# Reordering the tail of a mixer layer, and two projection products moved ahead of the head loop

## Chip, cores and metric

One NeuronCore of a Trainium2 chip runs the whole program. The metric is device time in microseconds; the span is that of one profiled execution. Engines: PE (TensorE), DVE (VectorE), ACT (ScalarE), POOL (GpSimd), and SP, which only issues DMAs here.

## The reference, cut to what matters

The program computes a first block (a mixer and a mixture of 64 experts) on 256 tokens of width 1024, then two layers of a second block. The change is in the mixer:

```python
glu_in, z, xbc, dt_raw, gate_in = split(n @ w_in)
u = a * sigmoid(b)                                    # a, b = halves of glu_in
u = silu(layernorm(causal_dwconv(u, cv_dw_w, cv_dw_b)))      # 31 taps: the long convolution
y_cv = u @ w_cv_out
y = ssd(silu(causal_dwconv(xbc)), softplus(dt_raw + dt_bias), ...) + d_skip * xh
y = rmsnorm_by_group(y * silu(z))                     # 4 groups of 512 channels
y_ssm = y @ w_ssm_out
g_cv, g_ssm = split(sigmoid(gate_in))
h = x + g1 * ((g_cv * y_cv + g_ssm * y_ssm) @ w_mix_out)
```

## The kernel before, in words

Every engine has one instruction stream, written out by hand, and waits on semaphores (`e.wait_ge(*k.at(name, n))`: the n-th result called name is there). All activations are kept with channels on the 128 partitions and the 256 tokens in the free dimension. Weights come in blocks of 2 MB into four slots of `ring` (block n goes to slot n % 4); the list `LOADS` (`mixer_loads`, L222) is the order in which `mixer_sp` (L259) issues them on SP, each behind the use of the block four places earlier. `k.at` with `mixer_used` says when a block has been used.

PE (`mixer_pe`, L341) first makes the products for b, a, x and dt (`product`: 16 matmuls of 128x256, since one f32 matmul shows as two in the trace). Behind dt, DVE and ACT compute softplus and running sums of the decay (L717 to L724, ACT L551 to L554); five transposes (L171) bring them to columns, and `prepare(0)` follows. Then comes a loop of 34 steps over the 32 heads: `decay`, `mix`, and at the steps of `fills_at` a "filler", one of the 32 products n = 0 to 31 of the z part (n < 16) and of the gates (n >= 16); they keep PE busy in the loop. Their eight weight blocks are called ("f", 0) to ("f", 7). The loop takes 26 fillers. Behind it PE does two fillers, the sum over channels that gives the long convolution's mean (`mean_sum`), filler 28, whose weights ("f", 7) are not in `LOADS` but second in `TAIL_LOADS`, eight sums of squares (`square_sum`, L194 and L201: ACT squares into one of two buffers, PE sums over partitions, and a third square waits until the first is summed), and three fillers. `z` is normalised on DVE by `norm(3)` (`inverse` L213, L772).

The tail is 24 products with 3 matmuls in place of each (`halved_product`, L487 to L489): operands are split into a high part (ACT, a copy to fp32r) and a low part (DVE, the difference), and high by high, low by high and high by low are added. Its weights come in eight pieces j of 2 MB: `tail_high` (ACT, L646) and `tail_low` (DVE, L655) split each piece in two instructions; piece j uses the buffers of piece j - 2, and load n waits for `tail_low` of piece n - 2 (semaphore "low"). Before, pieces 0 and 1 are w_cv_out (products 0 to 7), 2 to 5 w_ssm_out (8 to 15), 6 and 7 w_mix_out (16 to 23). Piece by piece, a w_cv_out or w_mix_out piece has 4 products of 8 k-tiles, a w_ssm_out piece 2 products of 16 k-tiles: 96 matmuls each. The operand halves are `uch`/`ucl` (ACT L602 silu, L603 copy; DVE L807 scaling, L803 difference), `zh`/`zl` (ACT L608, DVE L813) and `ych`/`ycl` (ACT L615, DVE L817). DVE multiplies each product by its gate (L830; L832 and L833 for the second branch) and adds the mix products to `h` (L837). Semaphores "mm_tail" count finished products, "tail" those taken out of PSUM; seven PSUM banks are used in turn (`Ring`).

Behind the tail come the root of the next norm, a router, and the experts: `moe_sp` issues 384 loads of 1 MB (L940), the first 12 without a use to wait for: four behind the semaphore "low" at 16, four behind product 20, four behind product 24 of the tail. The functions that the diff touches:

Of the kernel before, what the change touches and what calls it, by code (L numbers as in the profile page):

```python
# [7 lines left out]
F32 = mybir.dt.float32  # L8
# [208 lines left out]

def fills_at(h):
    return h % 4 != 3


def mixer_loads():  # L222
# [4 lines left out]
    out += [("x", blk) for blk in range(6)] + [("dt", 0)]  # L227
    n = 0
# [7 lines left out]
    return out  # L236
# [3 lines left out]
TAIL_LOADS = [("cv", 0), ("f", 7), ("cv", 1)] + [("ssm", i) for i in range(4)] + [("mix", i) for i in range(2)]  # L240
AFTER.update({f"layer_slot{i}": (f"slot{i}", 16 * len(LOADS[i::4])) for i in range(4)})
AFTER.update({f"ff_raw{i}": (f"raw{i}", 16 * len(TAIL_LOADS[i::2])) for i in range(2)})
TAIL_GROUPS = [4, 8, 10, 12, 14, 16, 20, 24]
# [15 lines left out]
def mixer_sp(k, e):  # L259
# [12 lines left out]
    for n in range(len(LOADS) - 4, len(LOADS)):  # L272
        if LOADS[n] != ("f", 6):
            e.wait_ge(*mixer_used(k, *LOADS[n]))
    for n, (what, i) in enumerate(TAIL_LOADS):
        if n == 0:
            e.wait_ge(*k.at("mm_f", 28))
        elif n == 2:
            e.wait_ge(*k.at("low", 2))
        elif n == 3:  # L280
            e.wait_ge(*k.at("mm_f", 32))
        elif n > 3:
            e.wait_ge(*k.at("low", 2 * (n - 2)))
        src = {"cv": lambda: w_tile(a["w_cv_out"], 0, 8, 512 * i, 512 * i + 512), "f": lambda: w_tile(w_in, 0, 8, 5152 + 512 * i, 5664 + 512 * i),
# [56 lines left out]
def mixer_pe(k, e, emptied):  # L341
# [39 lines left out]
    b = ring.take(("col", 0))  # L381
    e.wait_ge(*k.at("rest", 1))
    for i, x in enumerate((m_.dt[:, 0:128], m_.dt[:, 128:256], m_.cs[:, 0:128], m_.cs[:, 128:256], m_.rest)):
        ins = k.turn(e, k.pb[b][:, 32 * i:32 * i + 32], x, 32)
    ins.then_inc(k.s("dt_turned"), 1)
    ring.until(b, *k.at("col", 1))

# [3 lines left out]
    def filler():  # L391
# [4 lines left out]
        if n // 4 == 7:  # L396
            e.wait_ge(*k.at("raw1", 16))
            w = k.slot(1, [128, 8, 512])
        elif n % 4 == 0:
            w = mixer_slot(k, e, "f", n // 4, [128, 8, 512])  # L400
        else:
            w = k.slot(LOADS.index(("f", n // 4)) % 4, [128, 8, 512])
        b, ins = product(("f", n), w, 128 * (n % 4))
        ins.then_inc(k.s("mm_f"), 1)
        ring.until(b, *k.at("zg", n + 1))

# [62 lines left out]

# [4 lines left out]
    filler()  # L474
    for m in range(8):
        square_sum(k, e, SQ["ln"] + m, ROOT["ln"], m == 0, m == 7)
# [3 lines left out]
    def halved_product(n, w, c0, x, kt, late):  # L480
# [3 lines left out]
        for j in range(kt):  # L484
            if late:
                e.wait_ge(*k.at(late, j + 1))
# [6 lines left out]
    for j in range(8):  # L493
        e.wait_ge(*k.at("low", 2 * j + 2))
        if j < 2:
            w, x, cols, kt, late = halves(k, j, [8, 512]), (m_.ucl, m_.uch), 4, 8, "uc_low"
        elif j < 6:
            w, x, cols, kt, late = halves(k, j, [16, 256]), (m_.zl, m_.zh), 2, 16, None
            e.wait_ge(*k.at("z_low", 8))
# [2022 lines left out]
```

## Time and profile before

| what | us |
|---|---|
| median of 3 runs (2789.05 to 2794.97) | 2790.27 |
| the profiled execution, its own time | 2790.74 |
| its span | 2788.9 |
| PE busy (81%) | 2260.9 |
| DVE busy (37%) | 1031.4 |
| ACT busy (25%) | 693.8 |

The difference of 1.8 us between time and span lies outside the program's first and last instruction. Mean granted TensorE clock: 0.888 of full speed. The mixer is the first 532 us of the span, the experts the next 950 or so, the two layers the rest. In the rows further down a busy time is a sum over instructions, `xcount` the number merged into a row, and the bracket at the end the idle time of the engine before the row and what ended it.

### The profile page before, as it was taken

The page shows a single profiled execution, that of the slowest core. Times are in us where ns is not written, and L with a number is a line of the kernel's source. Part 1 is how long each engine was busy: PE and PEld are TensorE (multiplying, and loading weights), DVE is VectorE, ACT ScalarE, POOL GpSimd, SP SyncE. Part 2 cuts the span into 40 slices and gives each one's busy share as a digit, 9 for nine tenths or more (in the row PEclk, how much of TensorE's full clock was granted, in tenths as well). Part 3 has the DMA queues.
Part 4 walks back from the last instruction along what each step waited for, and adds up shares of the span by engine and source line. Part 5 has one row for each costly group of instructions (what it writes and reads, how often), then busy time and mean ns, then how long its engine had stood idle before and what let it go on. Part 6 is the DMA issues. An engine that isn't in the chain of part 4 may idle for free.

```text
span 2788.9 us, 31882 instructions
## 1 busy us (share of the span) xinstructions
PE 2260.9 (81%) x13027; PEld 1643.2 (59%) x13027; DVE 1031.4 (37%) x2106; ACT 693.8 (25%) x1057; POOL 27.3 (1%) x47
## 2 busy tenths in 40 slices
PE   7999989776666776666775887799999887799999
PEld 4876669732232333232331655578899655578899
DVE  1667736410000110010111356642653356632653
ACT  2135544300000000000001235322542235322542
POOL 0000000000000000000000100000000100000000
PEclk8999999888888888788888887899999988899999
DMA  8434516589999999999997131132453431132452
GB/s 303 151 123 151 181 61 204 193 352 421 422 421 421 421 421 422 420 422 420 418 421 305 46 114 46 61 146 96 152 182 109 130 115 45 61 143 99 151 182 106
DMA packets 174501, 631.45 MB, mean 226 GB/s; under 512 B 10816, under 2 KB 28768, under 8 KB 125200
## 3 DMA queue, kind: packets, MB, share of 16 engines
q1 hardware_dynamic: 173008, 628.07, 57.7%
q8 instruction: 106, 1.74, 0.3%
q0 software_dynamic: 1344, 1.28, 0.2%
q14 instruction: 43, 0.35, 0.0%
HBM read 628.28 MB, written 1.05 MB: 226 GB/s over the span
## 4 chain that ended last, share of the span: by engine, by line
PE 58%; DMA 27%; DVE 8%; ACT 3%; SPq 2%; issue 2%; DVEq 0%; ACTq 0%
PE pb L176 25%; DMA ring<-in_w 25%; PE pb L1779 5%; PE pb L1780 5%; PE pb L1781 5%; PE pb L1053 3%; PE pb L1027 3%; PE pb L1745 2%; SPq L940 1%; PE pb L1722 1%; PE pb L487 1%; PE pb L171 1%; PE pb L488 1%; PE pb L489 1%; PE pb L201 1%
## 5 line engine op out<-in xcount | busy, mean ns | idle before, releaser
L176 PE MATMUL pb<-ar,ring 128*128 128x256 f32 (+1 forms) x2960 | 708.1, 401 | 34.7 <-DMA ring<-in_w_in 16.1
L176 PEld LDWEIGHTS pb<-ar,ring 128*128 128x128 f32 (+1 forms) x2960 | 586.4, 200 | 156.5 <-issue 45.2
L1027 PE MATMUL pb<-ring,ar 128*32 128x512 f32 x2048 | 283.3, 710 | 127.7 <-DMA ring<-in_w 127.1
L1779 PE MATMUL pb<-act,parts 128*128 128x256 f32 x1152 | 332.2, 288 | 13.3 <-DVE act L2349 13.3
L1780 PE MATMUL pb<-act,parts 128*128 128x256 f32 x1152 | 328.4, 285 | 0.0
L1781 PE MATMUL pb<-act,parts 128*128 128x256 f32 x1152 | 328.1, 285 | 0.0
L1053 PE MATMUL pb<-ring,ar 128*32 128x512 f32 x1024 | 172.3, 834 | 120.0 <-DMA ring<-in_w 120.0
L1027 PEld LDWEIGHTS pb<-ring,ar 128*32 128x32 f32 x2048 | 77.0, 127 | 313.2 <-issue 312.5
L1779 PEld LDWEIGHTS pb<-act,parts 128*128 128x128 f32 x1152 | 222.4, 193 | 14.7 <-issue 14.1
L1780 PEld LDWEIGHTS pb<-act,parts 128*128 128x128 f32 x1152 | 222.3, 193 | 0.6
L1781 PEld LDWEIGHTS pb<-act,parts 128*128 128x128 f32 x1152 | 222.2, 193 | 0.0
L1859 DVE TENSOR_TENSOR parts<-ring,parts 128x2048 fp32r<-128x2048 f32 x72 | 161.7, 2287 | 128.6 <-ACT parts L1852 128.6
L1053 PEld LDWEIGHTS pb<-ring,ar 128*32 128x32 f32 x1024 | 46.6, 145 | 233.2 <-issue 229.5
L1246 DVE TENSOR_TENSOR ar<-ar,pb 128x512 f32<-128x512 f32 x16 | 11.0, 687 | 433.1 <-PE pb L1027 433.1
L1102 ACT ACTIVATE ar<-pb 128x512 f32<-128x512 f32 x16 | 9.6, 597 | 603.3 <-PE pb L1053 603.3
L1852 ACT ACTIVATE parts<-ring 128x2048 fp32r<-128x2048 f32 x72 | 133.5, 1901 | 96.3 <-PE pb L1781 83.3
L176 PE MATMUL pb<-ar 128*128 128x128 f32 x512 | 126.5, 421 | 35.3 <-DVE ar L1223 33.0
L176 PEld LDWEIGHTS pb<-ar 128*128 128x128 f32 x512 | 123.5, 335 | 50.0 <-DVE ar L1223 47.7
L1254 DVE COPY ar<-pb 128x512 f32<-128x512 f32 x16 | 11.1, 691 | 281.6 <-PE pb L1053 281.6
L695 DVE SCALAR_TENSOR_TENSOR ar<-ar,par 128x256 f32<-128x256 f32 x240 | 104.5, 475 | 0.0
L1096 ACT ACTIVATE ar<-pb 128x512 f32<-128x512 f32 x16 | 9.6, 597 | 318.8 <-PE pb L1027 318.8
L487 PE MATMUL pb<-act,parts 128*128 128x256 f32 x256 | 77.6, 303 | 8.4 <-DVE act L817 5.6
(339 smaller groups left out, 2483.3 us busy)
## 6 DMA issues: line engine op xcount, KB each, us to landing
ring<-in_w SPq DMA_DIRECT2D x384, 1024.0 KB, 18.6
ring<-in_w_in SPq DMA_DIRECT2D x36, 2048.0 KB, 7.9
ring<-in_w_ff SPq DMA_DIRECT2D x32, 2048.0 KB, 8.9
ring<-in_w_ada SPq DMA_DIRECT2D x12, 2048.0 KB, 13.0
ring<-in_w_ssm_out SPq DMA_DIRECT2D x4, 2048.0 KB, 8.8
ring<-in_w_out SPq DMA_DIRECT2D x4, 2048.0 KB, 7.7
ring<-in_w_cv_out SPq DMA_DIRECT2D x2, 2048.0 KB, 8.1
ring<-in_w_mix_out SPq DMA_DIRECT2D x2, 2048.0 KB, 7.7
```

The costliest lines, as they stand in the source:

```text
L171: return e.transpose(out, x, self.con("ident")[0:n, 0:n])
L176: ins = e.matmul(out, l, r, start=(i == 0), stop=(i == len(pairs) - 1))
L487: e.matmul(k.pb[b][:, 0:T], wh[:, j, c0:c0 + 128], xh[:, j, :], start=(j == 0), stop=False)
L695: made[m] = o.done(e.scalar_tensor_tensor(uc[:, m, :], ut[:, m, j:j + T], cw[:, m, j:j + 1], uc[:, m, :], ALU.mult, ALU.add), k.s("taps") ...
L1027: ins = e.matmul(k.pb[b][32 * j:32 * j + 32, :], v.xg[i][:, kt, 32 * j:32 * j + 32], w[j][:, m, :], start=(kt == 0), stop=(kt == 7))
L1053: ins = e.matmul(k.pb[yb[c]][32 * j:32 * j + 32, :], v.ht[i][:, kt, 32 * j:32 * j + 32], w[j][:, m, 512 * c:512 * c + 512], start=(kt == 0 ...
L1745: ins = e.matmul(k.pb[4][r0:r0 + 32, 0:T], v.ct[i][:, 2 * u + q, :], z[:, q, :], start=(j == 0), stop=(j == 3))
L1779: e.matmul(k.pb[b][:, 0:T], wh[:, kt, c0:c0 + 128], xh, start=(first and kt == 0), stop=False)
L1780: e.matmul(k.pb[b][:, 0:T], wl[:, kt, c0:c0 + 128], xh, start=False, stop=False)
L1781: ins = e.matmul(k.pb[b][:, 0:T], wh[:, kt, c0:c0 + 128], xl, start=False, stop=(last and kt == 7))
L1852: o.done(o.e.activation(high[:, 4 * i:4 * i + 4, :], raw[:, 4 * i:4 * i + 4, :], ACT.Copy), k.s("ff_high"))
L1859: o.done(o.e.tensor_tensor(low[:, 4 * i:4 * i + 4, :], raw[:, 4 * i:4 * i + 4, :], high[:, 4 * i:4 * i + 4, :].bitcast(F32), ALU.subtract) ...
```

## The change

Two fillers are issued between dt and the five transposes, on PE and ACT (`FIRST_FILLS`); `LOADS` gets ("f", 0) ahead of the first ada block and ("f", 7) at its end, so the other blocks come one place or more earlier and in other slots. The tail's pieces become w_ssm_out (0 to 3), w_cv_out (4, 5), w_mix_out (6, 7), so products 0 to 7 are those of the state-space output, with gates 8 to 15 of `g`. `zh` and `zl` are made ahead of the long convolution's norm; the eight sums of squares stand behind product 0 of the tail on PE; `uch`/`ucl` are made behind piece 2's split on ACT and DVE. The loads of pieces 0 and 1 wait for the last use of slots 0 and 1. On DVE `yc_low(7)` stands ahead of `tail_low(7)`.

```diff
--- before.py
+++ after.py
@@ -215,6 +215,10 @@
+
+FIRST_FILLS = 2
+
+
 def fills_at(h):
     return h % 4 != 3
 
@@ -224,8 +228,8 @@
     out = [("ada", blk) for blk in range(4)]
     for blk in range(2):
         out += [("b", blk), ("a", blk)]
-    out += [("x", blk) for blk in range(6)] + [("dt", 0)]
-    n = 0
+    out += [("x", blk) for blk in range(6)] + [("dt", 0), ("f", 0)]
+    n = FIRST_FILLS
     for h in range(34):
         if fills_at(h):
             if n % 4 == 0:
@@ -233,14 +237,18 @@
             n += 1
         if h % 4 == 0 and h < 32:
             out.append(("ada", 4 + h // 4))
-    return out
+    return out + [("f", 7)]
 
 
 LOADS = mixer_loads()
-TAIL_LOADS = [("cv", 0), ("f", 7), ("cv", 1)] + [("ssm", i) for i in range(4)] + [("mix", i) for i in range(2)]
+TAIL_LOADS = [("ssm", i) for i in range(4)] + [("cv", i) for i in range(2)] + [("mix", i) for i in range(2)]
 AFTER.update({f"layer_slot{i}": (f"slot{i}", 16 * len(LOADS[i::4])) for i in range(4)})
 AFTER.update({f"ff_raw{i}": (f"raw{i}", 16 * len(TAIL_LOADS[i::2])) for i in range(2)})
-TAIL_GROUPS = [4, 8, 10, 12, 14, 16, 20, 24]
+TAIL_GROUPS = [2, 4, 6, 8, 12, 16, 20, 24]
+
+
+def last_in_slot(i):
+    return LOADS[i::4][-1]
 
 
 def mixer_used(k, what, i):
@@ -269,19 +277,12 @@
         w = a["w_ada"] if what == "ada" else w_in
         e.dma_start(k.slot(n % 4, [128, 8, wide]), w_tile(w, 0, 8, c0, c0 + wide)).then_inc(k.s(f"slot{n % 4}"), 16)
 
-    for n in range(len(LOADS) - 4, len(LOADS)):
-        if LOADS[n] != ("f", 6):
-            e.wait_ge(*mixer_used(k, *LOADS[n]))
     for n, (what, i) in enumerate(TAIL_LOADS):
-        if n == 0:
-            e.wait_ge(*k.at("mm_f", 28))
-        elif n == 2:
-            e.wait_ge(*k.at("low", 2))
-        elif n == 3:
-            e.wait_ge(*k.at("mm_f", 32))
-        elif n > 3:
-            e.wait_ge(*k.at("low", 2 * (n - 2)))
-        src = {"cv": lambda: w_tile(a["w_cv_out"], 0, 8, 512 * i, 512 * i + 512), "f": lambda: w_tile(w_in, 0, 8, 5152 + 512 * i, 5664 + 512 * i),
+        if n < 2:
+            e.wait_ge(*mixer_used(k, *last_in_slot(n)))
+        else:
+            e.wait_ge(*k.at("low", 2 * n - 2))
+        src = {"cv": lambda: w_tile(a["w_cv_out"], 0, 8, 512 * i, 512 * i + 512),
                "ssm": lambda: w_tile(a["w_ssm_out"], 0, 16, 256 * i, 256 * i + 256),
                "mix": lambda: w_tile(a["w_mix_out"], 0, 8, 512 * i, 512 * i + 512)}[what]()
         e.dma_start(k.slot(n % 2, [128, 16, 256] if what == "ssm" else [128, 8, 512]), src).then_inc(k.s(f"raw{n % 2}"), 16)
@@ -378,31 +379,30 @@
     b, ins = product(("dt", 0), mixer_slot(k, e, "dt", 0, [128, 8, 32]), 0, 32)
     ins.then_inc(k.s("mm_dt"), 1)
     ring.until(b, *k.at("dt", 1))
+    fills = [0]
+    sums = []
+
+    def filler():
+        n = fills[0]
+        if n == 32:
+            return
+        fills[0] += 1
+        if n % 4 == 0:
+            w = mixer_slot(k, e, "f", n // 4, [128, 8, 512])
+        else:
+            w = k.slot(LOADS.index(("f", n // 4)) % 4, [128, 8, 512])
+        b, ins = product(("f", n), w, 128 * (n % 4))
+        ins.then_inc(k.s("mm_f"), 1)
+        ring.until(b, *k.at("zg", n + 1))
+
+    for _ in range(FIRST_FILLS):
+        filler()
     b = ring.take(("col", 0))
     e.wait_ge(*k.at("rest", 1))
     for i, x in enumerate((m_.dt[:, 0:128], m_.dt[:, 128:256], m_.cs[:, 0:128], m_.cs[:, 128:256], m_.rest)):
         ins = k.turn(e, k.pb[b][:, 32 * i:32 * i + 32], x, 32)
     ins.then_inc(k.s("dt_turned"), 1)
     ring.until(b, *k.at("col", 1))
-
-    fills = [0]
-    sums = []
-
-    def filler():
...
-        if n // 4 == 7:
-            e.wait_ge(*k.at("raw1", 16))
-            w = k.slot(1, [128, 8, 512])
-        elif n % 4 == 0:
...
 
     def prepare(grp):
         bm, cm = xa[:, 16 + grp, :], xa[:, 20 + grp, :]
@@ -466,14 +466,10 @@
     rest_of_sum(3)
     filler()
     filler()
-
     b = ring.take(("mean", 0))
     e.wait_ge(*k.at("taps", 8))
     k.group(e, k.pb[b][:, 0:T], [(k.con("ones"), uc[:, m, :]) for m in range(8)]).then_inc(k.s("mean_sum"), 1)
     ring.until(b, *k.at("mu", 1))
-    filler()
-    for m in range(8):
-        square_sum(k, e, SQ["ln"] + m, ROOT["ln"], m == 0, m == 7)
     while fills[0] < 32:
         filler()
 
@@ -483,7 +479,7 @@
         (wl, wh), (xl, xh) = w, x
         for j in range(kt):
             if late:
-                e.wait_ge(*k.at(late, j + 1))
+                e.wait_ge(*k.at(late, 8 * j // kt + 1))
             e.matmul(k.pb[b][:, 0:T], wh[:, j, c0:c0 + 128], xh[:, j, :], start=(j == 0), stop=False)
             e.matmul(k.pb[b][:, 0:T], wl[:, j, c0:c0 + 128], xh[:, j, :], start=False, stop=False)
             ins = e.matmul(k.pb[b][:, 0:T], wh[:, j, c0:c0 + 128], xl[:, j, :], start=False, stop=(j == kt - 1))
@@ -492,17 +488,19 @@
 
     for j in range(8):
         e.wait_ge(*k.at("low", 2 * j + 2))
-        if j < 2:
+        if j < 4:
+            w, x, cols, kt, late = halves(k, j, [16, 256]), (m_.zl, m_.zh), 2, 16, "z_low"
+        elif j < 6:
             w, x, cols, kt, late = halves(k, j, [8, 512]), (m_.ucl, m_.uch), 4, 8, "uc_low"
-        elif j < 6:
-            w, x, cols, kt, late = halves(k, j, [16, 256]), (m_.zl, m_.zh), 2, 16, None
-            e.wait_ge(*k.at("z_low", 8))
         else:
             w, x, cols, kt, late = halves(k, j, [8, 512]), (m_.ycl, m_.ych), 4, 8, "yc_low"
         for i in range(cols):
             n = (TAIL_GROUPS[j - 1] if j else 0) + i
             b = halved_product(n, w, 128 * i, x, kt, late)
             ring.until(b, *k.at("tail", n + 1))
+            if n == 0:
+                for m in range(8):
+                    square_sum(k, e, SQ["ln"] + m, ROOT["ln"], m == 0, m == 7)
             if n >= 18:
                 square_sum(k, e, SQ["h"] + n - 18, ROOT["h"], n == 18, False)
     for g in (6, 7):
@@ -552,7 +550,6 @@
     o.done(o.after().activation(m_.ex, m_.ex, ACT.Exp, scale=-1.0))
     o.done(o.after().activation(m_.ea, k.par("alog")[0:32, :], ACT.Exp))
     o.done(o.after().activation(m_.ex, m_.ex, ACT.Ln, bias=1.0), k.s("ln1p"))
-
     fills = [0]
 
     def filler():
@@ -573,6 +570,8 @@
             e.wait_ge(*k.at("yz", m + 1))
             square(k, o, z[:, m, :], SQ["y"] + m)
 
+    for _ in range(FIRST_FILLS):
+        filler()
     for h in range(34):
         if h < 32:
             e.wait_ge(*k.at("decay", h + 1))
@@ -586,28 +585,27 @@
         if h >= 10 and h % 8 == 2:
             grp = h // 8 - 1
             root(k, o, ROOT["y"] + grp, SQ["y"] + 4 * grp + 4, 512)
-    filler()
     root(k, o, ROOT["y"] + 3, SQ["ln"], 512)
+    tail_high(k, o, 0)
     filler()
     filler()
+    e.wait_ge(*k.at("zn", 16))
+    for i in range(8):
+        o.done(e.activation(m_.zh[:, 2 * i:2 * i + 2, :], z[:, 2 * i:2 * i + 2, :], ACT.Copy), k.s("z_high"))
+    filler()
+    filler()
+    tail_high(k, o, 1)
     for m in range(8):
         e.wait_ge(*k.at("centred", m + 1))
         square(k, o, uc[:, m, :], SQ["ln"] + m)
     root(k, o, ROOT["ln"], SQ["h"], D)
-    filler()
-    tail_high(k, o, 0)
-    filler()
+    tail_high(k, o, 2)
     for m in range(8):
         e.wait_ge(*k.at("uc_unit", m + 1))
         o.done(e.activation(uc[:, m, :], uc[:, m, :], ACT.Silu, scale=k.par("lng")[:, m:m + 1], bias=k.par("lnb")[:, m:m + 1]))
         o.done(o.after().activation(m_.uch[:, m, :], uc[:, m, :], ACT.Copy), k.s("uc_high"))
-    while fills[0] < 32:
-        filler()
-    e.wait_ge(*k.at("zn", 16))
-    for i in range(8):
-        o.done(e.activation(m_.zh[:, 2 * i:2 * i + 2, :], z[:, 2 * i:2 * i + 2, :], ACT.Copy), k.s("z_high"))
     for j in range(8):
-        if j < 7:
+        if 2 <= j < 7:
             tail_high(k, o, j + 1)
         for n in range(TAIL_GROUPS[j - 1] if j else 0, TAIL_GROUPS[j]):
             if 8 <= n < 16:
@@ -619,12 +617,11 @@
 
 
 def tail_raw(j):
-    n = j if j == 0 else j + 1
-    return n % 2, 16 * (n // 2 + 1)
+    return j % 2, 16 * (j // 2 + 1)
 
 
 def tail_shape(j):
-    return [16, 256] if 2 <= j < 6 else [8, 512]
+    return [16, 256] if j < 4 else [8, 512]
 
 
 def tail_high(k, o, j):
@@ -635,12 +632,13 @@
     o.e.wait_ge(*k.at(f"raw{slot}", landed))
     if j >= 2:
         o.e.wait_ge(*k.at("mm_tail", TAIL_GROUPS[j - 2]))
-    else:
+    elif j == 0:
 
         o.e.wait_ge(*k.at("mixed", 32))
         o.e.wait_ge(*k.at("ada_columns", 12))
-        o.e.wait_ge(*k.at("mm_f", 28))
-        o.e.wait_ge(*k.at("zn", 16))
+    else:
+        o.e.wait_ge(*mixer_used(k, *last_in_slot(2)))
+        o.e.wait_ge(*mixer_used(k, *last_in_slot(3)))
     s = shape[0] // 2
     for i in range(2):
         o.done(o.e.activation(high[:, s * i:s * i + s, :], raw[:, s * i:s * i + s, :], ACT.Copy), k.s("high"))
@@ -789,28 +787,25 @@
             norm(h // 8 - 1)
     run_taps(248)
     norm(3)
+    tail_low(k, o, 0)
+    for i in range(8):
+        e.wait_ge(*k.at("z_high", i + 1))
+        o.done(e.tensor_tensor(m_.zl[:, 2 * i:2 * i + 2, :], z[:, 2 * i:2 * i + 2, :], m_.zh[:, 2 * i:2 * i + 2, :].bitcast(F32), ALU.subtract), k.s("z_low"))
     e.wait_ge(*k.at("mean_sum", 1))
     mu = k.tiles(88, 1)[:, 0, :]
     o.done(o.after().tensor_scalar(mu, k.pb[k.bank["mean", 0]][:, 0:T], 1.0 / D, None, ALU.mult), k.s("mu"))
     o.after()
     for m in range(8):
         o.done(e.tensor_tensor(uc[:, m, :], uc[:, m, :], mu, ALU.subtract), k.s("centred"))
+    tail_low(k, o, 1)
     inv = inverse(k, o, ROOT["ln"])
-    tail_low(k, o, 0)
-
-    def uc_low(m):
-        e.wait_ge(*k.at("uc_high", m + 1))
-        o.done(e.tensor_tensor(m_.ucl[:, m, :], uc[:, m, :], m_.uch[:, m, :].bitcast(F32), ALU.subtract), k.s("uc_low"))
-
     o.after()
     for m in range(8):
         o.done(e.tensor_tensor(uc[:, m, :], uc[:, m, :], inv, ALU.mult), k.s("uc_unit"))
-        if m:
-            uc_low(m - 1)
-    uc_low(7)
-    for i in range(8):
-        e.wait_ge(*k.at("z_high", i + 1))
-        o.done(e.tensor_tensor(m_.zl[:, 2 * i:2 * i + 2, :], z[:, 2 * i:2 * i + 2, :], m_.zh[:, 2 * i:2 * i + 2, :].bitcast(F32), ALU.subtract), k.s("z_low"))
+    tail_low(k, o, 2)
+    for m in range(8):
+        e.wait_ge(*k.at("uc_high", m + 1))
+        o.done(e.tensor_tensor(m_.ucl[:, m, :], uc[:, m, :], m_.uch[:, m, :].bitcast(F32), ALU.subtract), k.s("uc_low"))
 
     def yc_low(m):
         e.wait_ge(*k.at("yc_high", m + 1))
@@ -818,18 +813,18 @@
 
     e.wait_ge(*k.at("zg", 32))
     for j in range(8):
-        if j < 7:
+        if j == 6:
+            yc_low(7)
+        if 2 <= j < 7:
             tail_low(k, o, j + 1)
         for n in range(TAIL_GROUPS[j - 1] if j else 0, TAIL_GROUPS[j]):
             acc = k.pb[k.bank["tail", n]][:, 0:T]
-            if n == 16:
-                yc_low(7)
             e.wait_ge(*k.at("mm_tail", n + 1))
             m = n % 8
             if n < 8:
-                o.done(e.tensor_tensor(m_.yc[:, m, :], acc, g[:, m, :], ALU.mult), k.s("tail"))
+                o.done(e.tensor_tensor(m_.yc[:, m, :], acc, g[:, 8 + m, :], ALU.mult), k.s("tail"))
             elif n < 16:
-                t = o.done(e.tensor_tensor(m_.tmp[:, m % 2, :], acc, g[:, n, :], ALU.mult), k.s("tail"))
+                t = o.done(e.tensor_tensor(m_.tmp[:, m % 2, :], acc, g[:, m, :], ALU.mult), k.s("tail"))
                 o.done(o.after(t).tensor_tensor(m_.yc[:, m, :], m_.yc[:, m, :], m_.tmp[:, m % 2, :], ALU.add), k.s("yc"))
                 if m:
                     yc_low(m - 1)
```

## Rows read from the trace of the kernel before

**Rows 1.** Busy time by stretch (columns first), stage of the experts.
```profile
core 0: us, PE busy (x) PEld busy (x) DVE busy (x) ACT busy (x) POOL busy (x), PEclk, DMA share, GB/s
600.00:650.00 50.00, 35.93 (x214) 17.53 (x214) 5.73 (x15) 1.58 (x3) 0.00 (x0) 0.83 1.01 421
```

**Rows 2.** Instructions in order of time, around dt.
```profile
183.76 2.11 PE L176 MATMUL pb<-ar,ring 128*32 128x256 f32 x9
192.68 0.71 PE L171 MATMUL pb<-const,ar 32*128 32x32 f32 x5 [6.82 <-DVE ar L724]
194.76 1.92 PE L171 MATMUL pb<-const,ar 128*128 128x128 f32 x8
...
227.16 1.04 PE L171 MATMUL pb<-const,ar 128*128 128x128 f32 x8
```

**Rows 3.** Busy time by stretch, behind dt.
```profile
192.60:196.60 4.00, 3.92 (x17) 3.38 (x17) 1.70 (x5) 0.00 (x0) 0.00 (x0) 0.50 0.57 211
```

**Rows 4.** Instructions in order of time, behind the loop over heads.
```profile
376.62 7.07 PE L176 MATMUL pb<-ar,ring 128*128 128x256 f32 x32
383.53 3.62 PE L176 MATMUL pb<-ar,const 128*128 128x256 f32 x16
384.20 0.59 SPq L287 DMA_DIRECT2D ring<-in_w_in  x1
396.97 6.14 PE L176 MATMUL pb<-ar,ring 128*128 128x256 f32 x16 [9.83 <-DMA ring<-in_w_in]
404.12 5.27 PE L201 MATMUL pb<-ar,const 128*128 128x256 f32 x16 [1.00 <-ACT ar L194]
409.22 10.52 PE L176 MATMUL pb<-ar,ring 128*128 128x256 f32 x48
421.73 0.36 PE L487 MATMUL pb<-act,parts 128*128 128x256 f32 x1 [1.98 <-DVE act L803]
```

**Rows 5.** Busy time by stretch, the squares' sums and the tail's products.
```profile
403.20:409.30 6.10, 5.00 (x17) 2.65 (x18) 0.00 (x0) 4.23 (x10) 0.00 (x0) 1.00 0.00 1
421.70:428.40 6.70, 6.41 (x22) 4.89 (x23) 4.87 (x13) 6.49 (x14) 0.00 (x0) 0.55 1.05 386
440.00:497.60 57.60, 57.60 (x480) 57.60 (x481) 32.86 (x38) 20.66 (x17) 0.00 (x0) 1.00 0.55 183
506.00:511.80 5.80, 5.80 (x29) 5.80 (x30) 0.52 (x2) 0.42 (x1) 0.00 (x0) 0.56 0.93 314
```

**Rows 6.** Instructions in order of time, the mix products.
```profile
498.82 0.42 ACT L615 ACTIVATE act<-ar 128x256 fp32r<-128x256 f32 x1 [3.53 <-DVE ar L833]
501.07 4.49 DVE L655 TENSOR_TENSOR parts<-ring,parts 128x2048 fp32r<-128x2048 f32 x2 [1.95 <-ACT parts L646]
505.95 0.58 PE L487 MATMUL pb<-act,parts 128*128 128x256 f32 x1 [5.58 <-DVE act L817]
514.64 0.48 DVE L837 SCALAR_TENSOR_TENSOR h<-pb,mod,h 128x256 f32<-128x256 f32 x1 [2.40 <-PE pb L489]
531.14 0.48 DVE L837 SCALAR_TENSOR_TENSOR h<-pb,mod,h 128x256 f32<-128x256 f32 x1 [2.82 <-PE pb L489]
```

**Rows 7.** Groups of instructions, 376 to 440 us (xcount | busy, mean ns | idle before).
```profile
L646 ACT ACTIVATE parts<-ring 128x2048 fp32r<-128x2048 f32 x5 | 9.3, 1902 | 2.3 <-PE pb L489 2.3
L655 DVE TENSOR_TENSOR parts<-ring,parts 128x2048 fp32r<-128x2048 f32 x4 | 9.0, 2288 | 3.4 <-ACT parts L646 3.4
L813 DVE TENSOR_TENSOR act<-ar,act 128x512 fp32r<-128x512 f32 x8 | 4.9, 686 | 1.8 <-ACT act L608 1.8
L602 ACT ACTIVATE ar<-ar,par 128x256 f32<-128x256 f32 x8 | 4.7, 587 | 1.6 <-DVE ar L807 1.6
L213 DVE RECIPROCAL ar<-ar 128x256 f32<-128x256 f32 x2 | 3.5, 1752 | 27.1 <-ACT ar L208 27.1
```

**Rows 8.** Instructions in order of time, start of the experts.
```profile
506.00 14.67 SPq L940 DMA_DIRECT2D ring<-in_w  x8
562.11 1.78 PE L1027 MATMUL pb<-ring,ar 128*32 128x512 f32 x8 [0.58 <-DVE ar L1231]
```

More of the change, by code:

```diff
@@ L380, in mixer_pe @@
     ring.until(b, *k.at("dt", 1))
[L381 to L386, printed above, removed]
     fills = [0]
@@ L405, in filler @@
         ring.until(b, *k.at("zg", n + 1))
+    for _ in range(FIRST_FILLS):
+        filler()
+    b = ring.take(("col", 0))
+    e.wait_ge(*k.at("rest", 1))
+    for i, x in enumerate((m_.dt[:, 0:128], m_.dt[:, 128:256], m_.cs[:, 0:128], m_.cs[:, 128:256], m_.rest)):
+        ins = k.turn(e, k.pb[b][:, 32 * i:32 * i + 32], x, 32)
+    ins.then_inc(k.s("dt_turned"), 1)
+    ring.until(b, *k.at("col", 1))
     def prepare(grp):
```

## The prediction

> **What bounds the kernel now.** I read the busy time by stretch first. In the stage of the experts the DMA share is 1.01 and 421 GB/s move while PE has gaps [rows 1]: that stage lasts as long as its loads. It can begin earlier, not run faster. The mixer, up to 532 us, is where the edit lies; there the DMA is far from full (183 GB/s in the tail's middle) and PE sets the pace: between 440.0 and 497.6 it ran 480 matmuls without a gap, 0.120 us each, at a granted clock of 1.00, the 2.4 GHz level [rows 5]. So in the mixer I looked for the places where PE stood or ran slow, in order of time, and read there what ended each wait. There are four.
>
> (a) Behind dt PE stands 6.82 us for the softplus chain on ACT and DVE (L724), and then the transposes and `prepare(0)` run from 192.6 to 196.6 at a clock of 0.50, the 1.2 GHz level [rows 2, 3]: eight transposes take 1.92 us against 1.04 in the next group [rows 2]. (b) Filler 28 waits 9.83 us for its weights, whose load was issued only at 384.20 and landed at 396.97; behind that wait the 16 matmuls take 6.15 us, where a product at full clock takes 3.45 ((383.53 - 376.62) / 2), and the first sum of squares waits another 1.00 [rows 4]. (c) The tail's first product waits 1.98 us for the operand halves of the long convolution, and its first piece then runs from 421.73 to 440.0 instead of 11.5 us, matmuls coming at the pace at which halves are made and at a clock of 0.55 [rows 4, 5]. (d) Inside the first mix product PE stands 5.58 us for `ycl` of tile 7, because DVE first ran `tail_low(7)` for 4.49 us; ACT had that tile's high half by 499.24. The next 5.8 us are at 0.56 [rows 5, 6].
>
> **The change part by part.** The work on PE is the same: 32 fillers, 16 sums, 24 products. Only its order and waits change, so I add up PE's stream.
>
> Two fillers ahead of the transposes. They cost 2 x 3.45 = 6.9 us of PE [rows 4] and start where dt's product ends, 185.9; they end at 192.8, and the transposes began at 192.68 before anyway [rows 2]. So they fill the wait, and 6.9 us leave the stretch behind the loop. ACT takes them out behind its last softplus step, so the chain itself is not lengthened. What is queued behind them is the first exp, which waits for PE's work after 194. Their weights, block f 0, are the first issued after dt's block in both kernels. With PE never idle, the 3.92 us at 0.50 [rows 3] should become 1.96: another 2.0 us. Bounds of this term: 0 if DVE rather than PE sets when the loop starts or the clock stays low, 2.0 if not; I take 2.0, since the loop's PE rows follow each other without long waits. Loop end: 376.6 - 2.0 = 374.7.
>
> Blocks of weights come one place earlier and in other slots. The nearest case is f 7: it waits for the use of f 5, whose last filler is now in step 28 of the loop, some 25 us before filler 28; a 2 MB load beside another took 12.8 us [rows 4]. The first state-space piece is queued right behind it and also lands ahead of its split. So 9.83 + (6.15 - 3.45) + 1.00 = 13.5 us go [rows 4]. If that cover were gone, PE would stand for what the load is late, as before.
>
> The tail's first piece. Behind the loop PE now does two fillers, the mean and two fillers without a wait: 374.7 + 6.9 + 3.4 + 6.9 = 391.9. By then `zh`, `zl` and piece 0 must be there. ACT: root, split of piece 0 (2 x 1.90), two gates, eight copies for `zh`, some 12 us from 375; DVE: the norm (the reciprocal alone 1.75; I allow 5 in all), `tail_low(0)` (2 x 2.29), eight differences (4.9) behind it [rows 7], hence about 389 for the last and 384 for the low half of the weights. PE asks for the first at 391.9, for the last 5 us later. So both the 2.16 us of standing (421.73 - 409.22 - 3 x 3.45) and the slow piece (440.0 - 421.73 - 11.52 = 6.75) go: 8.9 us [rows 4, 5]. The sixteen waits that each state-space product now has cost nothing I can see: the convolution's pieces had one to every three matmuls too, and 440.0 to 497.6, which holds both kinds, shows one pace [rows 5].
>
> The eight sums of squares move behind product 0: 5.1 us before (404.12 to 409.22), the same now, at most 1 us less [rows 4]. Their squares stand on ACT behind the split of piece 1, which waits for filler 31 and ends near 396; PE comes to them at 397.7, and DVE has centred `uc` by then.
>
> The long convolution's norm. It is now hidden: root near 404, reciprocal 1.75, scaling to 409; then ACT splits piece 2 when product 1 ends (408.5), 3.8 us, and makes eight pairs of silu and copy, 0.94 us a pair, to about 421.5 [rows 7]. DVE's `tail_low(2)` is done near 415.5, PE wants it at 408.5 + 11.5 = 420.0. `tail_low(3)` stands on DVE behind the last `ucl` and four gate products, done near 428, wanted at 431.5. This is the narrowest place, 3.5 us. What waits meanwhile is the emptying of the first four products' banks; there are seven, and the eighth product begins at about 437.
>
> The mix products. With `yc_low(7)` ahead, the half is ready at about 0.5 us behind ACT's, where the other tiles' were, before PE asks. Mix then takes 2 x 2.88 + 6 x 3.30 = 25.6 us, the 3.30 from (531.14 - 514.64) / 5, against 531.14 - 497.6 = 33.5: 7.9 us less [rows 5, 6]. `tail_low(7)` now ends 0.4 us later, needed 12 us after the mix begins.
>
> Behind the tail. The first loads of experts hang on "low" at 16, which comes at about 474.5 instead of 506.0 [rows 8], 31.5 earlier, while their first use comes 39 earlier. They had landed long before PE's first use at 562.11, 12 MB being 29 us at 421 GB/s [rows 1, 8]; the slack shrinks by 8 us and is not used up. So the rest of the program moves as a block.
>
> **Sum.** 6.9 + 2.0 + 13.5 + 8.9 + 7.9 = 39.2 us. Stepping through PE gives the same: 391.9 + 5.8 + 5.1 + 5.8 + 57.6 + 25.6 = 491.8 for the end of the last product, against 531.14. The profiled execution took 2790.74, 0.5 above the median: 2751.5 for such an execution, 2751 for the median of 2790.27.
>
> The granted clock at the sums of squares deserves a second look. Before, with 5.00 of 6.1 us busy and a gap behind every pair, it stayed at 1.00 [rows 5]. The Trainium skill, TensorE: Matmul & The Clock Gate, section A second HAM failure mode: psum-queue depth-cycling, says that frequent tiny idle times between groups of matmuls can make the clock swing between its levels; by that rule the sums inside the tail would drag product 1 down, and 2754 would come out. The row speaks against it.
>
> **Rivals.** (1) The clock falls at the sums: 29 matmuls at 0.56 took 5.8 us [rows 5], 2.3 more than at full clock: 2753.5. Against it, the row of the sums above. Chance 0.05. (2) A new wait at piece 3: the norm's chain is late by more than the 3.5 us of slack. Each us beyond costs one, and a stand like (d) adds its slow matmuls, 2.3. If ACT's pairs take 1.5 us instead of 0.94 because the two engines' queues interleave worse, it ends 4.5 later: 1 + 2.3, so 2755; up to 2760. For it, the chain is long and crosses both queues twice; against it, nothing else stands in them. Chance 0.10. (3) The experts' stream is bound from its first load, so only 31.5 us arrive: 2759. Against it, PE and the stream both stand until the first use. Chance 0.04. (4) DVE sets the loop, and the 2.0 us are not had: 2753. Chance 0.08. (5) Slower. One mechanism could do it: PE, now busy from dt to 492 us almost without a rest, is held at the 1.2 GHz level. It decides once 39 us of PE work run at half speed; for the 100 us from 392 on it would give 2751 + 100 = 2851. For it, every low level costs twice the time [rows 3]; against it, in every row at a low level PE had stood just before, and 57.6 us of solid work were at 1.00 [rows 3, 5]. Chance 0.01. That the change doesn't do what it says I give nothing; that the gain is lost somewhere I don't see, 0.02.
>
> **How the numbers follow.** That leaves 0.70 for the forecast itself, with 2748 to 2754 from the sums' 1 us, the start of the loop and a few tenths at each seam. The range takes in rivals 1 to 4 up to 2760, and 2746 below, since re-warming of the clock in the later layers can fall differently once everything moves. A measurement of this kernel tells about 0.2% (5.6 us) from no change. All cases but (5) and the unseen loss are over that: faster 0.97, same 0.02, slower 0.01.
>
> **What would show it.** Right: no wait at the transposes and clock 1.00 there; no DMA wait on PE between the loop and the tail; the tail's first matmul near 392 with clock 1.00 through to 492; no DVE wait in the first mix product; first use of the experts near 523. Wrong: a new wait of PE for the low half of piece 3's weights, a clock below 1 between 397 and 409, or a first use of the experts that waits for its load.

## The result, and the profile after

| what | before | after |
|---|---|---|
| median of the first comparison (4 runs each), us | 2790.62 | 2744.72 |
| its single runs, us | 2789.05 to 2794.97 | 2742.04 to 2745.85 |
| ratio, 95% interval | | 0.9832, 0.9815 to 0.9849 |
| the profiled execution, its own time / span, us | 2790.74 / 2788.9 | 2745.12 / 2743.3 |
| mean granted clock | 0.888 | 0.894 |

The changed kernel is 45.9 us faster. The forecast was 39.2 less, to 2751, with a range that ended at 2746: the direction was right, the gain came out 6.7 us larger, and the time lies 1.3 us under the range. Experiments e1 and e8 timed the same kernel again, five runs each: 2749.86 and 2747.61 against 2792.07 and 2790.62. Over these 14 runs of the changed kernel and the 28 of the one before beside them, the medians are 2747.3 and 2791.0: a gain of 43.7 us.

PE in order of time, kernel after, around dt and behind the loop over heads (idle time before a row and what ended it in brackets):

```profile
183.68 7.92 PE L176 MATMUL pb<-ar,ring 128*32 128x256 f32 x35
191.53 0.49 PE L171 MATMUL pb<-const,ar 32*128 32x32 f32 x5
192.71 1.04 PE L171 MATMUL pb<-const,ar 128*128 128x128 f32 x8
...
373.50 7.07 PE L176 MATMUL pb<-ar,ring 128*128 128x256 f32 x32
380.40 3.62 PE L176 MATMUL pb<-ar,const 128*128 128x256 f32 x16
383.86 7.07 PE L176 MATMUL pb<-ar,ring 128*128 128x256 f32 x32
390.57 0.47 PE L483 MATMUL pb<-act,parts 128*128 128x256 f32 x1
...
396.51 4.89 PE L201 MATMUL pb<-ar,const 128*128 128x256 f32 x16
```

The answer to [rows 2]: the two fillers run on from dt's product without a gap, the transposes have no idle time before them, and the eight of 128x128 take 1.04 us, where they took 1.92. The answer to [rows 4]: no wait for a load, none for the first square, none ahead of the tail's first product, which starts at 390.57 instead of 421.73. These are all the waits of PE from 180 to 520 us of the kernel after (columns: who waited for whom, us in total, times, longest):

```profile
PE pb L950 <- ACT ar L1076: 4.1, 1, 4.1
PE pb L176 <- issue: 2.5, 1, 2.5
PE pb L426 <- DVE ar L758: 2.3, 3, 0.8
PE pb L176 <- DVE ar L1159: 1.7, 1, 1.7
PE pb L438 <- issue: 1.4, 3, 0.5
PE pb L201 <- ACT ar L194: 0.7, 2, 0.5
```

Those of 9.8, 6.8, 5.6 and 2.0 us are gone, and nothing new stands in their place: the first, second and fourth rows belong to the router behind the tail. Busy time by stretch, kernel after, answering [rows 3, 5]:

```profile
192.60:196.60 4.00, 4.00 (x24) 3.24 (x23) 3.64 (x11) 1.65 (x3) 0.00 (x0) 1.00 0.17 61
396.50:401.10 4.60, 4.43 (x19) 2.44 (x17) 1.17 (x1) 2.85 (x7) 0.00 (x0) 1.00 0.50 162
401.10:472.00 70.90, 70.90 (x592) 70.87 (x591) 46.34 (x61) 35.41 (x39) 0.00 (x0) 1.00 0.40 139
```

PE's clock is 1.00, the 2.4 GHz level, through the transposes, through the sums of squares inside the tail, and through 592 matmuls without a gap, 0.120 us each, state-space products with their waits included. DVE and the last product of the tail, kernel after, answering [rows 6]:

```profile
465.59 0.99 DVE L812 TENSOR_TENSOR act<-ar,act 128x256 fp32r<-128x256 f32 x2
467.95 4.49 DVE L653 TENSOR_TENSOR parts<-ring,parts 128x2048 fp32r<-128x2048 f32 x2 [1.38 <-ACT parts L644]
...
490.15 0.48 DVE L832 SCALAR_TENSOR_TENSOR h<-pb,mod,h 128x256 f32<-128x256 f32 x1 [2.82 <-PE pb L485]
```

The low halves of tiles 6 and 7 are done before piece 7 is split. The last product is taken out at 490.15 instead of 531.14: 41.0 us earlier. Of these, 39.8 us lie between the first transpose and the last product (338.46 against 298.62); the other 1.2 were there when the transposes began (192.68 against 191.53), ahead of anything that the change touches.

So 41.0 of the 45.6 us by which the two spans differ were there at the tail's end. The other 4.6 came where the two programs are the same. The largest piece lies at one place, the last products that combine the experts. Kernel before, then after:

```profile
1501.39 5.11 PE L1053 MATMUL pb<-ring,ar 128*32 128x512 f32 x32 [4.95 <-DMA ring<-in_w]
1510.33 5.30 PE L1000 MATMUL pb<-ar 128*128 128x256 f32 x16 [3.82 <-issue]
1537.23 7.97 PE L176 MATMUL pb<-ar,ring 128*128 128x256 f32 x25 [11.67 <-DVE ar L2041]
```

```profile
1458.78 5.32 PE L1048 MATMUL pb<-ring,ar 128*32 128x512 f32 x32 [4.75 <-DMA ring<-in_w]
1466.82 3.72 PE L995 MATMUL pb<-ar 128*128 128x256 f32 x16 [2.73 <-issue]
1492.16 11.15 PE L176 MATMUL pb<-ar,ring 128*128 128x256 f32 x41 [11.68 <-DVE ar L2036]
```

The first row of each is 42.6 us apart, the second 43.5, the third 45.1: the same 16 matmuls took 5.30 us in one execution and 3.72 in the other. So 1.6 us came between the tail and these rows (0.9 of them by the experts' first use), 2.5 at this place, where the expectation of e1 says 3.3, and 0.5 behind it. The experiments had to say whether that belongs to the change.

### The profile page after: what moved, and what is told of

Read it like the earlier page. It is cut to its first block, busy times and chain, and to the rows that moved or that the text cites. A ratio compares the mean times of both kernels' runs of the same rounds, so it can differ in the third digit from the quotient of the medians.

```text
span 2743.3 us, 31878 instructions
## 1 busy us (share of the span) xinstructions
PE 2241.3 (82%) x13027; PEld 1631.5 (59%) x13027; DVE 1031.3 (38%) x2106; ACT 693.0 (25%) x1056; POOL 27.4 (1%) x47
## 4 chain that ended last, share of the span: by engine, by line
PE 59%; DMA 27%; DVE 8%; ACT 2%; SPq 2%; issue 2%; DVEq 0%; ACTq 0%
PE pb L176 26%; DMA ring<-in_w 26%; PE pb L1774 5%; PE pb L1775 5%; PE pb L1776 5%; PE pb L1048 3%; PE pb L1022 3%; PE pb L1740 2%; SPq L935 2%; PE pb L1717 1%; PE pb L484 1%; PE pb L485 1%; PE pb L483 1%; PE pb L171 1%; PE pb L201 1%
## 5 line engine op out<-in xcount | busy, mean ns | idle before, releaser
L176 PEld LDWEIGHTS pb<-ar,ring 128*128 128x128 f32 (+1 forms) x2960 | 584.4, 200 | 145.6 <-issue 45.6
L1774 PE MATMUL pb<-act,parts 128*128 128x256 f32 x1152 | 332.1, 288 | 13.3 <-DVE act L2344 13.3
L1775 PE MATMUL pb<-act,parts 128*128 128x256 f32 x1152 | 328.2, 285 | 0.0
L1776 PE MATMUL pb<-act,parts 128*128 128x256 f32 x1152 | 327.9, 285 | 0.0
L1774 PEld LDWEIGHTS pb<-act,parts 128*128 128x128 f32 x1152 | 223.6, 194 | 14.7 <-issue 14.1
L1249 DVE COPY ar<-pb 128x512 f32<-128x512 f32 x16 | 11.1, 692 | 284.0 <-PE pb L1048 284.0
L1872 ACT ACTIVATE ar<-pb,par 128x256 f32<-128x256 f32 x48 | 22.8, 474 | 220.8 <-PE pb L176 220.7
```

The lines of the kernel that those rows point to most:

```text
L176: ins = e.matmul(out, l, r, start=(i == 0), stop=(i == len(pairs) - 1))
L1774: e.matmul(k.pb[b][:, 0:T], wh[:, kt, c0:c0 + 128], xh, start=(first and kt == 0), stop=False)
L1775: e.matmul(k.pb[b][:, 0:T], wl[:, kt, c0:c0 + 128], xh, start=False, stop=False)
L1776: ins = e.matmul(k.pb[b][:, 0:T], wh[:, kt, c0:c0 + 128], xl, start=False, stop=(last and kt == 7))
```

## The experiments

All are compared with the kernel before, run beside them. Three marks are read in every trace: the first transpose behind dt (L171), the row of DVE that takes the tail's last product into `h` (L832, L837), and the end of the span.

**e1 and e2: both kernels again, unchanged.**

> The changed kernel once more, unchanged, for a tighter ratio and a second trace. What is asked is where the 4.6 us come from that the two traces differ by behind the tail's last product (2257.8 us before, 2253.2 after), about 1 us of it at the router and 3.3 at the last combine products of the experts, where the granted clock was 1.00 instead of partly 0.5. Theory A (luck of the clock's level in single executions): a new trace shows another time behind the tail, anywhere from 2251 to 2258, and the median gain of the larger sample settles near 40 to 42 us. Theory B (the edit itself shortens what follows): the time behind the tail is 2253 again, and the gain stays at 45 to 46.

> The kernel before once more, unchanged. Theory A: its time behind the tail differs from the first trace's 2257.8 by some us, and overlaps with the changed kernel's. Theory B: 2257 to 2258 again. Both: the ratio is 1.000 within 0.1%; how far single executions scatter shows what luck there is.

e1: 2749.86 us (2744.56 to 2752.2), ratio 0.9848 [0.9835, 0.9862], a gain of 42.2. e2: 2788.87 (2787.11 to 2793.74), ratio 0.9998 [0.9989, 1.0007]. Behind the tail the second trace of the changed kernel took 2748.1 - 490.6 = 2257.5 us, as long as the first trace of the kernel before (2257.8), and the second one of the kernel before took 2787.1 - 532.9 = 2254.2, nearly as little as the first of the changed (2253.2). Theory B is out. The same place in e1, the kernel after, and then in e2, the kernel before:

```profile
1467.39 5.41 PE L995 MATMUL pb<-ar 128*128 128x256 f32 x16 [2.18 <-issue]
1494.41 5.77 PE L176 MATMUL pb<-ar,ring 128*128 128x256 f32 x16 [11.68 <-DVE ar L2036]
```

```profile
1510.87 3.61 PE L1000 MATMUL pb<-ar 128*128 128x256 f32 x16 [3.00 <-issue]
1536.08 4.17 PE L176 MATMUL pb<-ar,ring 128*128 128x256 f32 x9 [11.67 <-DVE ar L2041]
```

The roles are swapped: from the first of these products to the next layer it is 27.0 us in e1 and 25.2 in e2. At this place it is the clock's level in the single execution, not the edit.

e2 held something else. Behind the same 6.8 us wait for dt its first filler ran at half speed. Kernel before, second execution, PE in order of time:

```profile
192.29 0.71 PE L171 MATMUL pb<-const,ar 32*128 32x32 f32 x5 [6.82 <-DVE ar L724]
194.37 1.91 PE L171 MATMUL pb<-const,ar 128*128 128x128 f32 x8
196.22 1.22 PE L426 MATMUL pb<-ar,const 32*128 32x256 f32 x2
197.36 6.04 PE L176 MATMUL pb<-ar,ring 128*128 128x256 f32 x16
```

and the stretch behind it, in e2 and in the first trace of the kernel before:

```profile
196.00:200.00 4.00, 4.00 (x10) 2.68 (x9) 3.38 (x10) 1.61 (x2) 0.00 (x0) 0.50 0.00 0
```

```profile
196.00:200.00 4.00, 4.00 (x18) 3.02 (x17) 3.67 (x10) 1.51 (x2) 0.00 (x0) 0.86 0.00 0
```

In the first trace the low level ended early in that stretch, in e2 it lasted through it. From the transposes to the loop's end it is 183.9 us in the first trace and, by the same rows, 186.6 in e2; in the changed kernel 182.0. So behind the same wait the slow clock cost 2.0 us once and 4.6 another time.

**e3: the tile's low half late again.**

```diff
     for j in range(8):
-        if j == 6:
-            yc_low(7)
         if 2 <= j < 7:
             tail_low(k, o, j + 1)
+        if j == 6:
+            yc_low(7)
```

> The changed kernel with the low half of the last yc tile behind the split of piece 7 again, as before the change: this undoes one part. My sum gives that part 7.9 us: PE waits 5.6 us inside the first mix product and runs some 5 us at the lower clock. So about 2752.5 us against 2744.7. A rival says that the wait is worth nothing when the rest is early, since the experts' stream sets the end: then 2745 to 2746.

2755.5 us (2754.22 to 2756.37), ratio 0.9874 [0.9859, 0.9889]. The wait is back, in the waits of PE of this kernel:

```profile
PE pb L483 <- DVE act L812: 5.6, 1, 5.6
```

From the transposes to the tail's end: 306.3 us against 298.6, so 7.7, forecast 7.9. The rival, that it is worth nothing, is out. (In absolute time the expectations of e3 and e4 count from 2744.7, the first and lowest sample of the changed kernel; that is why their medians lie 3 and 5 us above them.)

**e4: no fillers ahead of the transposes.**

```diff
-FIRST_FILLS = 2
+FIRST_FILLS = 0
...
-            if n % 4 == 0:
+            if n and n % 4 == 0:
                 out.append(("f", n // 4))
...
-    filler()
-    filler()
+    while fills[0] < 32:
+        filler()
```

> The changed kernel without the two fillers ahead of the transposes: they go behind the mean (six products between loop and tail), all else as changed. My sum gives the part 6.9 + 2.0 = 8.9 us: about 2753.5. In the trace PE stands 6.8 us at the transposes and the 17 matmuls behind it take 3.9 us at 0.50. Rival: the term for the clock is not had, because DVE sets the loop's start: 6.9, 2751.6.

2758.36 us (2755.71 to 2761.13), ratio 0.9884 [0.9869, 0.9899]. From the transposes to the tail's end 307.5 us: 8.9 more than 298.6, forecast 8.9. This trace has the short low level, 0.53 from 192 to 196 us and 1.00 behind:

```profile
192.00:196.00 4.00, 4.00 (x15) 3.25 (x14) 2.33 (x6) 0.00 (x0) 0.00 (x0) 0.53 0.36 134
196.00:200.00 4.00, 4.00 (x21) 3.11 (x24) 2.90 (x9) 1.92 (x3) 0.00 (x0) 1.00 0.00 0
```

The median is 11.1 above 2747.3; 8.9 in some executions and 11.5 in others would give that, which one trace can't show. (`filler` in the second half of the diff is ACT's, behind `zh`.)

**e5: block f 7 late.**

```diff
         if n >= 4:
             e.wait_ge(*mixer_used(k, *LOADS[n - 4]))
+        if (what, i) == ("f", 7):
+            e.wait_ge(*k.at("mm_f", 28))
```

> The changed kernel, with the load of block f 7 held back until filler 27 is done, as before the change: this undoes the part on loads. It is issued at about 370.5 in the trace's time, with no other load beside it it should land in 8 to 9 us, and PE wants it at 373.9: a wait of some 5 to 6 us, 2.5 for the lower clock behind it; the two loads of the state-space weights queue behind it, and piece 0's split comes some 5 us late, which PE does not feel. My sum gave this part 13.5 us with a second load beside it and the first square's wait in it; here I expect 7.5 to 9, so a tail end near 498 and 2755. Rival: the delay is taken up by slack in ACT and DVE later and nothing is lost; tail end 490.

2757.36 us (2755.57 to 2757.61), ratio 0.9878 [0.9863, 0.9893]. PE and SP of this kernel in order of time:

```profile
381.68 9.26 PE L176 MATMUL pb<-ar,ring 128*128 128x256 f32 x32 [5.53 <-DMA ring<-in_w_in]
...
373.20 0.37 SPq L280 DMA_DIRECT2D ring<-in_w_in  x1
```

The load took 8.5 us with no other ahead of it, where it had taken 12.8 behind another in the kernel before; PE waited 5.53 instead of 9.83, and the two products behind it took 2.2 more than 7.07. From the transposes to the tail's end it is 306.5, 7.9 above the changed kernel, as expected; the transposes began at 194.03 in this trace, hence a tail's end of 500.5 and not 498. The rival, slack that takes the delay up, is out: there is none in the PE stream.

**e6: the tail's order undone, the other parts kept.**

```diff
-TAIL_LOADS = [("ssm", i) for i in range(4)] + [("cv", i) for i in range(2)] + [("mix", i) for i in range(2)]
-TAIL_GROUPS = [2, 4, 6, 8, 12, 16, 20, 24]
+TAIL_LOADS = [("cv", i) for i in range(2)] + [("ssm", i) for i in range(4)] + [("mix", i) for i in range(2)]
+TAIL_GROUPS = [4, 8, 10, 12, 14, 16, 20, 24]
...
     filler()
+    for m in range(8):
+        square_sum(k, e, SQ["ln"] + m, ROOT["ln"], m == 0, m == 7)
     while fills[0] < 32:
         filler()
```

and the same sums taken out from behind product 0, with ACT and DVE in the order of the kernel before. The loads of pieces 0 and 1 stay as early as in the changed kernel.

> The changed kernel with the tail's order undone: long convolution first, its norm and the eight sums between the fillers as before, but f 7 in time, two fillers ahead of the transposes and yc tile 7 early. If the parts add up as in my sum, this costs 8.9 us: tail end 499, about 2756. Against that, the wait for f 7 in the kernel before covered part of the norm's chain: from the root to the tail's first product it takes 11.7 us, the root now comes at about 393, so PE would stand some 9 us instead of 2 and run the slow piece too: tail end near 506, 16 us above the changed kernel, about 2762.

2760.92 us (2758.58 to 2762.43), ratio 0.989 [0.9875, 0.9905]. PE in order of time:

```profile
393.51 3.62 PE L176 MATMUL pb<-ar,ring 128*128 128x256 f32 x16
404.95 0.55 PE L486 MATMUL pb<-act,parts 128*128 128x256 f32 x1 [7.83 <-DVE act L800]
```

and the first piece behind it, by stretch:

```profile
405.50:412.30 6.80, 6.80 (x25) 5.29 (x24) 5.30 (x14) 6.61 (x15) 0.00 (x0) 0.50 0.77 252
```

The tail ends at 505.5. From the transposes to there it is 312.75 us: 14.1 above the changed kernel, where the sum by parts said 8.9 and the chain's length 16. The wait for f 7, which used to cover part of the norm's chain, is gone, so PE stands 7.8 us instead of 2.0 at the tail. The sum had split the gain wrongly: it gave 13.5 to f 7 and 8.9 to the tail's order, and undone alone they cost 7.9 (e5) and 14.1. Together that is 22.0, close to the sum's 22.4. Seen from the kernel before, a punctual f 7 alone would have brought about 9 us and not 13.5, since 14 of the 23 us that the two parts bring together would still have been lost at the tail.

**e7: the kernel before, with the tile's low half early.**

```diff
     for j in range(8):
+        if j == 6:
+            yc_low(7)
         if j < 7:
             tail_low(k, o, j + 1)
...
-            if n == 16:
-                yc_low(7)
```

> The kernel before, with one part of the change alone: the low half of yc tile 7 ahead of the split of piece 7. My sum gives it 7.9 us: tail end 523 instead of 530.8 to 532.6, about 2783 against 2791. Rival (needs the rest of the change): no gain.

2782.07 us (2778.51 to 2783.82), ratio 0.9965 [0.9952, 0.9979]: 8.6 us less than 2790.62. From the transposes to the tail's end 332.9 us, against 340.6 in e2, whose low level behind dt was as long: 7.7. This part needs none of the others.

**e8: the changed kernel a third time.**

> The changed kernel a third time. Theory A (level of the clock by luck): tail end 490 again within half a us, but the time behind it anywhere in 2253 to 2258 as in the six traces so far, whichever kernel; gain over the runs of before 41 to 46. Theory B is out if the time behind the tail is above 2255 again.

2747.61 us (2747.13 to 2749.87), ratio 0.9846 [0.9833, 0.986], a gain of 43.0. Here my expectation for the tail's end missed: 492.5, not 490. But the transposes also begin 2.4 us later, at 193.91, ahead of anything the change touches, and from there to the tail's end it is 298.6 us, as in the two traces before (298.6 and 298.6). The 2.4 us are there from the start of the mixer's long row of products, at 41.90 instead of 39.47. Busy time by stretch, first and third trace of the changed kernel:

```profile
30.00:50.00 20.00, 14.46 (x67) 11.12 (x68) 3.75 (x11) 6.09 (x13) 0.70 (x1) 0.74 1.04 387
```

```profile
30.00:50.00 20.00, 14.64 (x56) 10.63 (x57) 3.75 (x11) 5.57 (x11) 0.70 (x1) 0.57 1.05 387
```

The granted clock is 0.74 in one and 0.57 in the other: the clock's level once more. Behind the tail it is 2255.6.

**e9 and e10: one and three fillers ahead of the transposes** (FIRST_FILLS = 1 and 3 in e4's kernel).

> The changed kernel with one filler ahead of the transposes instead of two (five products between loop and tail, the third one behind the mean). PE stands 3.4 us at the transposes. The traces so far say that a stand of 6.8 us brings the low level, and that it then costs 2.0 us in two executions and 4.6 in two others. If a stand of 3.4 us does not bring it: +3.4, time from the transposes to the tail's end 301.7 instead of 298.3. If it does: 303.7 or 306.3.

> The changed kernel with three fillers ahead of the transposes. PE reaches the transposes 3.4 us later, with the clock high, and has one product less behind the loop: a PE stream without gaps has the same length, so the tail ends within 0.5 us of the changed kernel, about 2747. Rival: PE comes early to the tail's operands (zl is done only 4 us ahead of the tail now) and waits, 1 to 3 us more with the low level.

e9: 2755.76 us (2753.71 to 2757.16), ratio 0.9872 [0.9856, 0.9887]. PE in order of time:

```profile
192.45 0.71 PE L171 MATMUL pb<-const,ar 32*128 32x32 f32 x5 [3.17 <-DVE ar L722]
194.53 1.92 PE L171 MATMUL pb<-const,ar 128*128 128x128 f32 x8
```

Behind a stand of 3.17 us the clock was at the 1.2 GHz level too, and it was the long one: 306.7 us to the tail's end, 8.1 more than with two fillers, 3.45 of them the product that moved and 4.6 the clock. Whether every execution drops there isn't known from one trace.

e10: 2746.17 us (2743.38 to 2748.33), ratio 0.9835 [0.9822, 0.9849]. From the transposes to the tail's end 295.1, and 295.1 + 3.45 = 298.6: the same PE stream, no wait at the tail. Two fillers are what the wait holds, a third brings nothing that these runs can tell.

## Why the prediction missed, point by point

**The parts.** In the table the forecast stands beside what a trace of this study shows for the same part.

| part | forecast, us | shown, us |
|---|---|---|
| two fillers into dt's wait | 6.9 | 6.9 (e4, less 2.0 for the clock) |
| slow clock behind that wait | 2.0 | 2.0 (first trace, e4), 4.6 (e2, e7, and e9) |
| f 7, with what follows it | 13.5 | 7.9 undone alone (e5) |
| tail's order | 8.9 | 14.1 undone alone (e6) |
| f 7 and tail's order together | 22.4 | 23.1 to 23.3 (22.6 to 22.8 against e2) |
| yc tile 7 | 7.9 | 7.7 (e3, e7) |
| from the transposes to the tail's end, fillers' 6.9 in it | 39.2 | 39.8 (338.46 - 298.62), 42.0 (340.60 - 298.62) |

The fifth row is the difference from the loop's end to the tail's end, 531.14 - 376.62 = 154.52 before and 490.15 - 373.50 = 116.65 after, 37.9 us, less the 6.9 of the fillers and 7.7 to 7.9 of the tile. Most of what is over are the sums of squares, which I left at 5.1 us and which take 4.5 inside the tail (396.51 to 401.05), because the first two squares are ready when PE comes.

**The step that failed** is the bound on the slow clock behind dt: "Bounds of this term: 0 if DVE rather than PE sets when the loop starts or the clock stays low, 2.0 if not". The 2.0 was half of the 3.92 us that the one trace showed as slow in the window I had cut, and I took it as the most that could be had. It was the least: with the same stand before it, the low level cost 2.0 us in two traces and 4.6 in two others. If the two are equally common, which four traces can't tell, the middle of the term is 3.3 (an estimate) and the sum 40 to 41. In the profiled pair itself the term came out as forecast, 183.94 - 181.97 = 2.0. There the spans differ by 6.4 us more than the sum says, and only 0.6 of it lies between the transposes and the tail's end; 1.2 lies ahead of them and 4.6 behind the tail.

**The second step that failed** turns the sum into a time: "So the rest of the program moves as a block", with 5 us left below the forecast. It is right in that no trace shows anything there that depends on the change. But the same instructions behind the tail took 2253.2 to 2257.8 us over the twelve traces, with no order by kernel (before 2257.8, 2254.2; changed 2253.2, 2257.5, 2255.6; the other seven 2254.0 to 2257.5), and the transposes began at 191.3 to 194.0, though nearly the same time lies between dt's product and them in all but e10. The medians of the three samples of the changed kernel are 5.1 us apart, 2744.72 to 2749.86. The pooled median, 2747.3, lies 3.7 us under the forecast and inside the range, like the two later samples; the first four runs lay another 2.6 lower, and that part of the miss was the luck of a sample. The pooled gain of 43.7 is 1.7 to 3.9 us above the 39.8 to 42.0 that the traces place between the transposes and the tail's end. The 14 runs spread over 10 us (2742.04 to 2752.2), which leaves some 2 us either way on that gain, so this rest may be scatter; no run here shows whether anything else is in it.

**The rivals.** (1) The clock did not fall at the sums: 1.00 from 396.5 to 401.1 with 4.43 of 4.60 us busy. The rule of the Trainium skill (TensorE: Matmul & The Clock Gate, A second HAM failure mode: psum-queue depth-cycling) is not borne out at this place: tiny idle times between pairs of sums left the level alone. (2) No new wait at piece 3. These rows of DVE in the kernel after hold the last `ucl`, the first four gate products and the split of piece 3's weights, one behind the other:

```profile
419.96 0.43 DVE L808 TENSOR_TENSOR act<-ar,act 128x256 fp32r<-128x256 f32 x1 [0.52 <-ACT act L606]
420.30 1.41 DVE L825 TENSOR_TENSOR ar<-pb,ar 128x256 f32<-128x256 f32 x4
421.77 4.50 DVE L653 TENSOR_TENSOR parts<-ring,parts 128x2048 fp32r<-128x2048 f32 x2
```

The split ends at 426.3 and PE comes to piece 3 at 430.0, when the 288 matmuls of the first three pieces are through: 3.7 us to spare, forecast 3.5. (3) The experts' first use came 41.9 us earlier, at 520.18, and waited for no load, although their first load, at 472.89, was only 33.1 earlier (506.00 before). (4) DVE does not set the loop; PE has the same three waits of 0.8 us in it in both kernels. (5) PE stayed at the upper level from dt to the tail's end.

## What to carry to other kernels

Where one engine works through a fixed list, add up its stream from the point where it last waited, and look for each wait's successor: here the wait for a load had covered part of a norm's chain, and taking away only the one would have left 14 of the 23 us standing in the other. Moving a small, long-waited piece ahead of a large one in an in-order queue, as the low half of one tile ahead of a weight split, was worth 7.7 us here, over half of what reordering the tail was, and needs nothing else. The four waits of PE removed here, of 2.0 to 9.8 us, had each cost their length and then a slow stretch; behind the one at dt that stretch's length differed from one execution to the next. So take such a stretch from several traces, or leave room for more than twice what one shows. And before setting a range, time the unchanged kernel several times in small samples: how far their medians lie apart is the least that the range has to leave on each side.

## What the runs showed of the hardware

The same 6.8 us stand of PE, ended at the same instruction, was followed by a low level worth 2.0 us in two traces and 4.6 in two others, and a stand of 3.17 us brought it too, worth 4.6. The tail's first product of the kernel before had waited only 1.98 us when the low level came (0.55 from 421.7 to 428.4), with a further short wait for the operand halves behind it; the waits of 0.8 us in the loop left the clock at 1.00. Where PE hardly stood, the timing repeated to a few hundredths: 298.62, 298.59 and 298.61 us from the transposes to the tail's end in three executions, and 298.6 again with a product moved in e10. Between runs the whole program scatters by some 7 us (2786.83 to 2793.78 in 15 runs of the kernel before), and the twelve traces find it in several stretches: 191.3 to 194.0 us ahead of the transposes and 25.2 to 27.2 between the last combine products and the next layer, both read above as the clock's level, but also 975.2 to 979.2 from the tail's end to those products and 1251.0 to 1254.6 from the next layer to the end. What sets the last two isn't read here.
